# Odd heads of a two-block kernel: outputs with tokens on partitions, and each head's gate row loaded instead of multiplied out

## The chip, the cores and the metric

The kernel runs on one core of one Trainium2 chip. The metric is the device time of one execution in microseconds; less is better. Engines are named as in the profile: PE is TensorE, DVE is VectorE, ACT is ScalarE, POOL is GpSimd, and SP issues most of the DMA transfers.

## The reference, cut to what matters

The whole kernel computes two transformer blocks, with a second block of an even and an odd layer. The change is in the odd layer, an mLSTM with 8 heads, 512 tokens in 4 chunks of 128, 128 channels for q and k and 256 for v. Per head and chunk:

```
b = cumsum(lf);  m_t = running maximum;  g_inter = exp(b + m_prev - m_t)
sc  = (q k^T) * exp(b_t - b_s + li_s - m_t), causal
num = g_inter * (q C) + sc v
den = g_inter * (q n) + sum_s sc
hout = num / max(|den|, exp(-m_t))
C, n = decay * C + kw^T v,  decay * n + sum kw
...
y = rmsnorm over the head's 256 channels(hout) * norm * sigmoid(og) * silu(z)
```

All of it is in fp32. `og`, `z`, `v`, `q`, `k` and the two gates come from one projection of the normalised input.

## The kernel before, in words

`odd_stage` runs the projection and the heads together. `Projection` (class in the same file) turns the weights into products: a job is 128 output columns over 16 row blocks, each with three fp32r products of 512 tokens (high times high, high times low, low times high), 48 products. Weights come in chunks of four row blocks, four chunks to such a job, through a ring of six slots: SP loads a chunk up to 12 chunks ahead, ACT makes its high part (`split_high`, L2400), DVE its low part (`split_low`, L2407), PE multiplies (L2384 to L2386). A slot is free again when PE has used it (`chunk_done`) and, for the raw weights, when the low part is made (`lo_set`).

The first 21 jobs (`EARLY`) make q, k, the gate rows and v, which go through DRAM. Then each head has four jobs, two for `og` and two for `z`, and PE's order of work is written out by hand: a job, then the head's first products, a job, the state products, a job, the output products, a job, the sums. So the head's own work on DVE, ACT and POOL has a job of PE's time to finish in.

In the head's first piece PE multiplies table columns, repeated by a step of zero, with the identity. That lays one row of the table over all partitions, in PSUM: `b - m` to bank 0 (L3996, `cum_ready`) and `m` to bank 1 (`m_ready`). ACT makes `grow` and `floor` from them, DVE `expo`. PE also turns k (L4001) and multiplies k with q (L4005). The state products (L4013, L4014) are 256 columns of v and 128 columns of ones for each of three chunks. The output products (L4024, L4026) put channels on partitions and 512 tokens on columns: one bank for the denominator, repeated on all partitions by a stationary `ones`, and two for the numerator. ACT and DVE make the denominator's absolute value, maximum and reciprocal on 128 x 512, and the quotient `o`; ACT squares it; PE sums the squares over the channels with two products with `ones` (L4040); ACT makes the inverse root, DVE multiplies by it and the norm, then by the gate that POOL made from `og` and `z`, and SP stores the head.

SP loads k, q and v of the next head during the current one (`load`, L3926 to L3928), into two buffers in turn. In the last head `tail.turn_p` and the tail's first weights are fitted between; the tail's (`Tail.tensor`) third embedding job waits until the head's banks 0 and 1 are free.

A table load on ACT (`preload_act_table_set` and before L2419) comes wherever the function changes between the set with exponential and logarithm and the sets with sigmoid and silu.

Of the kernel before, what the change touches and what calls it, by code (L numbers as in the profile page):

```python
# [1223 lines left out]
ML_SW = (ML_E + 1) * P  # L1224
# [2607 lines left out]
def odd_stage(nc, a, consts, cols, h, qk_dram, v_dram, y_dram, sum_sq, lead, following, p_tok, p_in, u, make_tail):  # L3832
# [8 lines left out]
    SW = ML_SW  # L3841
    GATE_JOB, EARLY, PER_HEAD = 2, 21, 4
    FIRST_LOAD, FIRST_MADE = 18, (0, 9, 17)
    ADD_BANK = (3, 0, 1)
    with ExitStack() as ctx:
# [9 lines left out]
        v_tok = [sb("v_tok0", ML_CH, ML_E * P)]  # L3855
        q_in, k_in = ([sb(f"{n}_in0", LAT)] for n in "qk")
        inv, inv_col, eps = sb("inv", LAT), sb("inv_col", ML_CH), sb("eps", 1)
        tabs = sb("tabs", ML_TABS, ML_CH, ML_H)
        og, z = sb("og", ML_E, LAT), sb("z", ML_E, LAT)
# [9 lines left out]
        for head in range(ML_H):  # L3869
            free = (y_set, head) if head > 0 else None  # L3870
# [16 lines left out]
        def rows8(name, *shape):  # L3887
# [11 lines left out]
        v_tok = [v_tok[0], sb("v_tok1", ML_CH, ML_E * P, owner=late)]  # L3899
        grow, expo, floor = sb("grow", ML_CH, P, owner=late), sb("expo", ML_CH, P, owner=late), sb("floor", LAT, owner=late)  # L3900
        score, k_w, state = sb("score", ML_CH, P, owner=late), sb("k_w", ML_CH, P, owner=late), sb("state", ML_CH - 1, SW, owner=late)
        den, o_sq, o, o_inv = sb("den", LAT, owner=late), sb("o_sq", ML_E, LAT, owner=late), sb("o", ML_E, LAT, owner=late), sb("o_inv", LAT, owner=late)
# [5 lines left out]
        cum_ready, m_ready, k_turned, kq_ready = sem("cum_ready"), sem("m_ready"), sem("k_turned"), sem("kq_ready")  # L3908
        grow_set, floor_set, expo_set, w_set = sem("grow_set"), sem("floor_set"), sem("expo_set"), sem("w_set")
        q_grown, k_w_set, score_set = sem("q_grown"), sem("k_w_set"), sem("score_set")  # L3910
        add_ready, state_set = sem("add_ready"), sem("state_set")
        den_ready, num_ready = sem("den_ready"), sem("num_ready")
        den_abs, den_max, den_inv, o_set = sem("den_abs"), sem("den_max"), sem("den_inv"), sem("o_set")
        o_squared, o_sums, o_ln, o_inv_set, y_normed, gate_set, y_gated = (sem(n) for n in (
            "o_squared", "o_sums", "o_ln", "o_inv_set", "y_normed", "gate_set", "y_gated"))
# [3 lines left out]
        def _(sp):  # L3919
# [4 lines left out]
            def load(hd):  # L3924
                b = hd % 2
                sp.dma_start(k_in[b][:], qk_dram[hd + ML_H]).then_inc(loaded[b], 16)  # L3926
                sp.dma_start(q_in[b][:], qk_dram[hd]).then_inc(loaded[b], 16)
                sp.dma_start(v_tok[b][:], v_view[:, :, ML_E * P * hd:ML_E * P * (hd + 1)]).then_inc(loaded[b], 16)  # L3928

            for n in range(EARLY):  # L3930
                proj.sp_upto(sp, KD * (n + 1))
                if n == FIRST_LOAD:
                    for made in FIRST_MADE:
                        proj.wait_job_stored(sp, made)
                    load(0)
                if n == GATE_JOB:
                    sp.wait_ge(proj.evacuated, n + 1)
                    for i in range(2):
                        sp.dma_start(raw_gates[:, i, :], gate_rows[112 + 8 * i:120 + 8 * i, :]).then_inc(gate_moved, 16)
            for hd in range(ML_H):  # L3940
                for j in range(PER_HEAD):
                    proj.sp_upto(sp, KD * (EARLY + PER_HEAD * hd + j + 1))
                    if j == 1 and hd < ML_H - 1:
                        if hd == 0:
                            proj.wait_stored(sp)
                        else:
                            sp.wait_ge(q_grown, hd)
                            sp.wait_ge(num_ready, ML_E * hd)
# [9 lines left out]
                sp.wait_ge(y_set, hd + 1)  # L3958
# [6 lines left out]
        def _(pe):  # L3965
# [19 lines left out]
            for hd in range(ML_H):  # L3985
# [25 lines left out]
                pe.wait_ge(floor_set, hd + 1)  # L4011
# [8 lines left out]
                for i, e, ready in ((2, ML_E, den_ready), (3, 0, num_ready), (0, 1, num_ready)):  # L4020
                    for c in range(ML_CH):
                        part = slice(c * P, (c + 1) * P)
                        if c > 0:
                            pe.matmul(bank[i][:, part], state[:, c - 1, e * P:(e + 1) * P], grow[:, c, :], start=True, stop=False)  # L4024
                        values = ones[:] if e == ML_E else v_tok[hd % 2][:, c, e * P:(e + 1) * P]
                        last = pe.matmul(bank[i][:, part], values, score[:, c, :], start=(c == 0), stop=True)  # L4026
                    last.then_inc(ready, 1)
# [15 lines left out]

        @block.scalar
        def _(act):
            norm.act(act)
            for n in range(EARLY):
# [9 lines left out]
                if n == GATE_JOB + 6:  # L4057
                    act.wait_ge(gate_n, 15)
                    act.preload_act_table_set(EXP_LN)
                    act.activation(tabs[:, 4:6, :, :], tabs[:, 4:6, :, :], ACT.Exp).then_inc(tabs_set, 1)  # L4060

            for hd in range(ML_H):
# [3 lines left out]
                act.wait_ge(cum_ready, hd + 1)  # L4066
                if hd > 0:
                    act.wait_ge(num_ready, ML_E * hd)
# [11 lines left out]
                act.wait_ge(den_ready, hd + 1)  # L4080
                act.activation(den[:], bank[2][:, :], ACT.Abs).then_inc(den_abs, 1)
                if hd == ML_H - 1:
                    tail.p_high(act, 0, bank[1])
                act.wait_ge(o_set, ML_E * (hd + 1))
                act.activation(o_sq[:], o[:], ACT.Square).then_inc(o_squared, 1)
                if hd == ML_H - 1:
                    tail.p_high(act, 1, bank[1])
# [710 lines left out]
```

## Time and profile before

| | us |
|---|---|
| median of 3 runs | 3729.44 |
| lowest, highest run | 3723.15, 3731.35 |
| profiled execution, span from first to last instruction | 3723.4 |
| the eight odd heads in it | 2878 to 3325 |

For the profiled execution no other time than its span is given. An fp32 product appears in the trace as two records of PE, and a transpose as one. The records' lengths overlap, since products are pipelined, so the cost of a product is the distance between starts, or its part of the chain that ended last. "Idle before" is the time in which an engine did nothing before an instruction, and the arrow names what released it.

### The profile page before, as it was taken

To read this page: it belongs to the slowest core of one execution; us is meant where nothing else is said; L and a number is where in the kernel's file an instruction comes from. 1 tells how busy PE (TensorE), PEld (TensorE's weight loads), DVE (VectorE), ACT (ScalarE), POOL (GpSimd) and SP (SyncE) were. 2 spreads that over 40 slices of the span, in tenths; PEclk is the share of its full clock that TensorE was granted. 3 is DMA by queue.
4 is the path that set the end of the run, shared out by engine and by line. 5 is a ranking of instruction groups with operands and counts; after the bars stand their busy time and mean duration, and the time that the engine had idled before them with its cause. 6 is when DMAs were issued, how large, how long until landed. Compare 5 with 4: busy or idle time off the path is not lost. (4 is left out here: it accounts for less than half of the span.)

```text
span 3723.4 us, 49664 instructions
## 1 busy us (share of the span) xinstructions
PE 3550.2 (95%) x19794; PEld 2945.9 (79%) x19794; DVE 1956.4 (53%) x2995; ACT 1512.3 (41%) x2540; POOL 422.1 (11%) x346
## 2 busy tenths in 40 slices
PE   6999999899878889999999999999999999999998
PEld 3688888777667777888888788888888888888886
DVE  7555554466578545645555554445533444454543
ACT  3322222255646543556565532333322444452332
POOL 1000000044000000001011160120000000024021
PEclk8999999999989999999999999999999999999999
DMA  9743333322544354422322253335634555543332
GB/s 358 264 141 127 112 106 107 93 79 80 173 127 119 96 171 133 145 83 79 94 86 88 79 176 96 95 79 115 132 116 122 125 95 112 105 133 102 94 94 88
DMA packets 580504, 448.37 MB, mean 120 GB/s; under 512 B 64454, under 2 KB 500114, under 8 KB 579504
## 3 DMA queue, kind: packets, MB, share of 16 engines
q1 hardware_dynamic: 570416, 420.98, 40.3%
q10 hardware_dynamic: 7712, 19.34, 1.3%
q0 software_dynamic: 2144, 4.87, 0.4%
q8 instruction: 157, 2.57, 0.3%
q14 instruction: 75, 0.61, 0.1%
HBM read 387.61 MB, written 57.46 MB: 120 GB/s over the span
## 5 line engine op out<-in xcount | busy, mean ns | idle before, releaser
L2407 DVE TENSOR_TENSOR w_lo<-w,w_hi 128x512 fp32r<-128x512 f32 x429 | 291.4, 698 | 499.7 <-ACT w_hi L2400 499.7
L2400 ACT ACTIVATE w_hi<-w 128x512 fp32r<-128x512 f32 x429 | 261.0, 625 | 478.5 <-PE od_acc L2386 179.0
L4539 DVE TENSOR_TENSOR w_lo<-w,w_hi 128x512 fp32r<-128x512 f32 x260 | 232.2, 899 | 353.3 <-ACT w_hi L4432 351.9
L4398 PE MATMUL ta_acc<-u_hi,w_hi 128*128 128x512 f32 x960 | 375.2, 391 | 2.7 <-POOL u_lo L4333 1.4
L4400 PE MATMUL ta_acc<-u_hi,w_lo 128*128 128x512 f32 x960 | 373.7, 389 | 0.0
L4399 PE MATMUL ta_acc<-u_lo,w_hi 128*128 128x512 f32 x960 | 373.5, 389 | 0.0
L4432 ACT ACTIVATE w_hi<-w 128x512 fp32r<-128x512 f32 x260 | 163.5, 630 | 440.4 <-PE ta_acc L4400 435.0
L2384 PE MATMUL od_acc<-u_hi,w_hi 128*128 128x512 f32 x768 | 304.7, 397 | 0.0
L2386 PE MATMUL od_acc<-u_hi,w_lo 128*128 128x512 f32 x768 | 299.3, 390 | 0.0
L2385 PE MATMUL od_acc<-u_lo,w_hi 128*128 128x512 f32 x768 | 299.0, 389 | 0.0
L2384 PE MATMUL ev_acc<-u_hi,w_hi 128*128 128x512 f32 x608 | 250.7, 412 | 13.7 <-DVE w_lo L2407 5.1
L2386 PE MATMUL ev_acc<-u_hi,w_lo 128*128 128x512 f32 x608 | 239.2, 393 | 0.0
L2385 PE MATMUL ev_acc<-u_lo,w_hi 128*128 128x512 f32 x608 | 239.1, 393 | 0.0
L1969 PE MATMUL p_acc<-u_hi,p_w_hi 128*128 128x512 f32 x544 | 216.9, 399 | 2.5 <-DVE p_w_lo L1777 2.5
L1976 PE MATMUL p_acc<-u_hi,p_w_lo 128*128 128x512 f32 x544 | 216.9, 399 | 0.0
L4398 PEld LDWEIGHTS ta_acc<-u_hi,w_hi 128*128 128x128 f32 x960 | 180.2, 188 | 43.0 <-DVE u_lo L4547 3.0
L1970 PE MATMUL p_acc<-u_lo,p_w_hi 128*128 128x512 f32 x544 | 213.3, 392 | 0.0
L4400 PEld LDWEIGHTS ta_acc<-u_hi,w_lo 128*128 128x128 f32 x960 | 180.2, 188 | 37.8
L4399 PEld LDWEIGHTS ta_acc<-u_lo,w_hi 128*128 128x128 f32 x960 | 180.2, 188 | 37.7 <-issue 0.5
L2113 DVE TENSOR_TENSOR p_w_lo<-p_w,p_w_hi 128x1024 fp32r<-128x1024 f32 x66 | 80.6, 1224 | 225.9 <-ACT p_w_hi L2015 225.9
L2015 ACT ACTIVATE p_w_hi<-p_w 128x1024 fp32r<-128x1024 f32 x66 | 69.7, 1060 | 249.7 <-PE p_acc L1976 179.9
L2385 PEld LDWEIGHTS od_acc<-u_lo,w_hi 128*128 128x128 f32 x768 | 144.3, 188 | 30.9 <-issue 1.9
(754 smaller groups left out, 7973.2 us busy)
## 6 DMA issues: line engine op xcount, KB each, us to landing
w<-in_o_w_in_dram SPq DMA_DIRECT2D x260, 256.0 KB, 6.7
w<-in_e_w_in_dram SPq DMA_DIRECT2D x144, 256.0 KB, 2.9
p_w<-in_w_in_dram SPq DMA_DIRECT2D x70, 512.0 KB, 6.1
mod_w<-in_w_ada_dram SPq DMA_DIRECT2D x32, 1024.0 KB, 11.4
w<-in_ple_gate_w_dram SPq DMA_DIRECT2D x128, 256.0 KB, 2.7
gate_w<-in_w_ada_dram SPq DMA_DIRECT2D x16, 1024.0 KB, 5.9
z_w<-in_w_in_dram SPq DMA_DIRECT2D x64, 256.0 KB, 3.0
w<-in_e_w_out_dram SPq DMA_DIRECT2D x64, 256.0 KB, 2.7
```

Of the source, the lines that this page charges most:

```text
L1969: pe.matmul(lat, wh, x_hi[:, k, :], start=first, stop=False)
L1970: pe.matmul(lat, wh, x_lo[:, k, :], start=False, stop=False)
L1976: last = pe.matmul(lat, wl, x_hi[:, k, :], start=False, stop=end)
L2384: pe.matmul(out, hi, self.x_hi[:, k, :], start=first, stop=False)
L2385: pe.matmul(out, hi, self.x_lo[:, k, :], start=False, stop=False)
L2386: last = pe.matmul(out, lo, self.x_hi[:, k, :], start=False, stop=end)
L2400: act.activation(self.w_hi[m % self.ring][:], self.w[m % self.ring][:], ACT.Copy).then_inc(self.hi_set, 1)
L2407: eng.tensor_tensor(self.w_lo[m % self.ring][:], self.w[m % self.ring][:], self.w_hi[m % self.ring][:].bitcast(F32), ALU.subtract).then_in ...
L4398: pe.matmul(bank, hi, hi_x[:, k, :], start=(k == 0), stop=False)
L4399: pe.matmul(bank, hi, lo_x[:, k, :], start=False, stop=False)
L4400: last = pe.matmul(bank, lo, hi_x[:, k, :], start=False, stop=(k == job.kd - 1))
L4539: dve.tensor_tensor(self.w_lo[m % RING][:], self.w[m % RING][:], self.w_hi[m % RING][:].bitcast(F32), ALU.subtract).then_inc(self.lo_set, 1)
```

## The change

The output products change sides: `grow` and `score` are stationary, and the state or v with one column of ones (`SW` = 257) is moving. Their results have tokens on partitions, one bank to a chunk (`NUM_BANK`), the denominator in column 256. The denominator's maximum and reciprocal are then on one column a chunk; ACT squares and sums along the row in one instruction a chunk, and the inverse root is on four columns. DVE scales each chunk into `y_tok`, PE turns it back (8 transposes), and DVE multiplies by the norm and the gate out of PSUM. The state products take the column of ones with v. The rows `b - m` are stored to DRAM once, and each head's row is loaded repeated over the partitions (`cum_in`) with k, q and v. `floor` is made once for all heads. `turn_p` in the last head uses the projection's banks, the gate on POOL is made in two halves, and the tail's third embedding job waits for the last head's `y_set`; the tail's second `embed_odd_out` moves behind it.

```diff
--- before.py
+++ after.py
...
-ML_SW = (ML_E + 1) * P
+ML_SW = ML_E * P + 1
...
+    NUM_BANK = (2, 3, 0, 1)
...
-        v_tok = [sb("v_tok0", ML_CH, ML_E * P)]
+        v_tok = [sb("v_tok0", ML_CH, SW)]
...
+        cum_in = [sb("cum_in0", LAT)]
+        cum_dram = nc.dram_tensor("s_cum3", (ML_H, LAT), F32).ap()
...
+        y_tok, squares = sb("y_tok", ML_CH, ML_E * P, owner=late), sb("squares", ML_CH, ML_E * P, owner=late)
...
             def load(hd):
                 b = hd % 2
+                sp.dma_start(cum_in[b][:], cum_dram[hd:hd + 1, :].to_broadcast([P, LAT])).then_inc(loaded[b], 16)
...
+                sp.dma_start(v_tok[b][:, :, 0:ML_E * P], v_view[:, :, ML_E * P * hd:ML_E * P * (hd + 1)]).then_inc(loaded[b], 16)
...
+                    sp.wait_ge(cum_stored, 16)
...
+                if n == GATE_JOB + 4:
+                    sp.wait_ge(gate_n, 8)
+                    sp.dma_start(cum_dram[:, :], rows[:, 0, :]).then_inc(cum_stored, 16)
...
-                else:
-                    pe.wait_ge(o_set, ML_E * hd)
-                    pe.wait_ge(o_ln, hd)
-                for i, t, ready in ((0, 0, cum_ready), (1, 2, m_ready)):
-                    for c in range(ML_CH):
-                        last = pe.matmul(bank[i][:, c * P:(c + 1) * P], tabs[:, t, c, hd:hd + 1].to_broadcast([P, P]),
-                                         ident[:], start=True, stop=True)
-                    last.then_inc(ready, 1)
...
-                pe.wait_ge(loaded[hd % 2], 48 * (hd // 2 + 1))
+                pe.wait_ge(loaded[hd % 2], 64 * (hd // 2 + 1))
...
+                if hd > 0:
+                    pe.wait_ge(y_set, ML_E * hd)
                 for c, i in enumerate(ADD_BANK):
-                    pe.matmul(bank[i][:, 0:ML_E * P], k_w[:, c, :], v_tok[hd % 2][:, c, :], start=True, stop=True)
-                    pe.matmul(bank[i][:, ML_E * P:SW], k_w[:, c, :], ones[:], start=True, stop=True).then_inc(add_ready, 1)
+                    pe.matmul(bank[i][:, 0:SW], k_w[:, c, :], v_tok[hd % 2][:, c, :], start=True, stop=True).then_inc(add_ready, 1)
...
+                for c, i in enumerate(NUM_BANK):
+                    if c > 0:
+                        pe.matmul(bank[i][:, 0:SW], grow[:, c, :], state[:, c - 1, :], start=True, stop=False)
+                    pe.matmul(bank[i][:, 0:SW], score[:, c, :], v_tok[hd % 2][:, c, :], start=(c == 0), stop=True).then_inc(num_ready, 1)
...
-                        if f > 0:
-                            pe.wait_ge(tail.p_set, f)
-                        tail.turn_p(pe, f, bank[1])
+                        tail.turn_p(pe, f, proj.acc[f][1])
                         proj.pe_steps(pe, KD // 2)
-                    pe.wait_ge(tail.p_set, 2)
-                pe.wait_ge(o_squared, hd + 1)
+                pe.wait_ge(y_tok_set, ML_CH * (hd + 1))
                 for e in range(ML_E):
-                    last = pe.matmul(bank[1][:, :], ones[:], o_sq[:, e, :], start=(e == 0), stop=(e == ML_E - 1))
-                last.then_inc(o_sums, 1)
-            tail.tensor(pe, None, (o_ln, ML_H))
+                    for c in range(ML_CH):
+                        last = pe.transpose(bank[e][:, c * P:(c + 1) * P], y_tok[:, c, e * P:(e + 1) * P], ident[:])
+                    last.then_inc(y_turned, 1)
+            tail.tensor(pe, None, (y_set, ML_E * ML_H))
...
+                    act.activation(floor[:], tabs[:, 2, :, :], ACT.Exp, scale=-1.0).then_inc(floor_set, 1)
...
-                act.wait_ge(cum_ready, hd + 1)
+                act.wait_ge(loaded[hd % 2], 64 * (hd // 2 + 1))
...
-                    ins = act.activation(grow[:, c, :], bank[0][:, c * P:(c + 1) * P], ACT.Exp, bias=tabs[:, 7, c, hd:hd + 1])
+                    ins = act.activation(grow[:, c, :], cum_in[hd % 2][:, c * P:(c + 1) * P], ACT.Exp, bias=tabs[:, 7, c, hd:hd + 1])
                 ins.then_inc(grow_set, 1)
-                act.wait_ge(m_ready, hd + 1)
-                act.activation(floor[:], bank[1][:, :], ACT.Exp, scale=-1.0).then_inc(floor_set, 1)
...
-                act.wait_ge(den_ready, hd + 1)
-                act.activation(den[:], bank[2][:, :], ACT.Abs).then_inc(den_abs, 1)
...
+                    tail.p_high(act, 0, proj.acc[0][1])
+                act.preload_act_table_set(EXP_LN)
+                act.wait_ge(den_inv, hd + 1)
+                if hd > 0:
+                    act.wait_ge(scale_set, hd)
+                for c, i in enumerate(NUM_BANK):
+                    ins = act.activation(squares[:, c, :], bank[i][:, 0:ML_E * P], ACT.Square, scale=den[:, c:c + 1], accum_out=y_sq[:, c:c + 1])
+                ins.then_inc(squared, 1)
+                act.wait_ge(squared, hd + 1)
+                act.activation(y_scale[:], y_sq[:], ACT.Ln, scale=1.0 / (ML_E * P), bias=eps[:, 0:1]).then_inc(y_ln, 1)
+                act.wait_ge(y_ln, hd + 1)
+                act.activation(y_scale[:], y_scale[:], ACT.Exp, scale=-0.5).then_inc(y_inv_set, 1)
...
-                act.preload_act_table_set(EXP_LN)
-                act.wait_ge(o_sums, hd + 1)
-                act.activation(o_inv[:], bank[1][:, :], ACT.Ln, scale=1.0 / (ML_E * P), bias=eps[:, 0:1]).then_inc(o_ln, 1)
-                act.wait_ge(o_ln, hd + 1)
-                act.activation(o_inv[:], o_inv[:], ACT.Exp, scale=-0.5).then_inc(o_inv_set, 1)
...
+                for e in range(ML_E):
+                    pool.wait_ge(proj.finished, proj.finish_no[EARLY + PER_HEAD * hd + 2 + e])
+                    pool.tensor_tensor(z[:, e, :], og[:, e, :], z[:, e, :], ALU.mult).then_inc(gate_set, 1)
...
-                dve.tensor_tensor(expo[:], bank[0][:, :].rearrange("p (c t) -> p c t", c=ML_CH),
+                dve.tensor_tensor(expo[:], cum_in[hd % 2][:].rearrange("p (c t) -> p c t", c=ML_CH),
...
-                dve.wait_ge(den_abs, hd + 1)
-                dve.tensor_tensor(den[:], den[:], floor[:], ALU.max).then_inc(den_max, 1)
...
+                for c, i in enumerate(NUM_BANK):
+                    dve.wait_ge(num_ready, ML_CH * hd + c + 1)
+                    ins = dve.tensor_scalar(den[:, c:c + 1], bank[i][:, ML_E * P:SW], floor[:, c, hd:hd + 1], None, ALU.max)
+                ins.then_inc(den_max, 1)
+                dve.wait_ge(den_max, 2 * hd + 1)
+                for c, i in enumerate(NUM_BANK):
+                    ins = dve.scalar_tensor_tensor(den[:, c:c + 1], bank[i][:, ML_E * P:SW], -1.0, den[:, c:c + 1], ALU.mult, ALU.max)
+                ins.then_inc(den_max, 1)
+                dve.wait_ge(den_max, 2 * hd + 2)
+                dve.reciprocal(den[:], den[:]).then_inc(den_inv, 1)
                 if hd == ML_H - 1:
-                    tail.p_low(dve, 0, bank[1])
-                dve.wait_ge(den_max, hd + 1)
-                dve.reciprocal(den[:], den[:]).then_inc(den_inv, 1)
...
+                    tail.p_low(dve, 0, proj.acc[0][1])
+                dve.wait_ge(y_inv_set, hd + 1)
+                dve.tensor_tensor(y_scale[:], y_scale[:], den[:], ALU.mult).then_inc(scale_set, 1)
+                dve.wait_ge(scale_set, hd + 1)
+                for c, i in enumerate(NUM_BANK):
+                    dve.tensor_scalar(y_tok[:, c, :], bank[i][:, 0:ML_E * P], y_scale[:, c:c + 1], None, ALU.mult).then_inc(y_tok_set, 1)
...
-                    tail.embed_odd_out(dve, 1)
-                dve.wait_ge(o_inv_set, hd + 1)
+                dve.wait_ge(stored, 16 * hd)
                 for e in range(ML_E):
-                    ins = dve.scalar_tensor_tensor(o[:, e, :], o[:, e, :], norm_w[:, ML_E * hd + e:ML_E * hd + e + 1], o_inv[:],
-                                                   ALU.mult, ALU.mult)
-                ins.then_inc(y_normed, 1)
-                dve.wait_ge(y_normed, hd + 1)
-                dve.wait_ge(gate_set, hd + 1)
-                dve.tensor_tensor(o[:], o[:], z[:], ALU.mult).then_inc(y_set, 1)
+                    dve.wait_ge(y_turned, ML_E * hd + e + 1)
+                    dve.wait_ge(gate_set, ML_E * hd + e + 1)
+                    dve.scalar_tensor_tensor(o[:, e, :], bank[e][:, :], norm_w[:, ML_E * hd + e:ML_E * hd + e + 1], z[:, e, :],
+                                             ALU.mult, ALU.mult).then_inc(y_set, 1)
+            tail.embed_odd_out(dve, 1)
```

## Rows read from the trace of the kernel before

**Rows 1.** The page's head and its first part: engine, busy us, share, instructions.

```profile
span 3723.4 us, 49664 instructions
...
PE 3550.2 (95%) x19794; PEld 2945.9 (79%) x19794; DVE 1956.4 (53%) x2995; ACT 1512.3 (41%) x2540; POOL 422.1 (11%) x346
```

**Rows 2.** Busy table by stretches: us, busy us, granted clock (PEclk), DMA share, GB/s.

```profile
2999.16:3054.30 55.14, 55.14 (x279) 46.42 (x278) 24.70 (x33) 24.28 (x38) 3.69 (x2) 1.00 0.52 103
2878.00:3325.00 447.00, 447.00 (x2255) 376.23 (x2254) 200.11 (x269) 194.39 (x306) 29.50 (x16) 1.00 0.54 112
```

**Rows 3.** PE's waits in the eight heads, 2880 to 3330 us.

```profile
PE ta_acc L4398 <- ACT od_o_inv L4095: 0.5, 1, 0.5
```

**Rows 4.** The chain that ended last, one head: start us, us, what.

```profile
2999.32 1.78 PE od_bank L3996 x16
3001.10 0.44 PE od_bank L4001 x4
3001.54 0.89 PE od_bank L4005 x8
...
3003.13 0.23 PE od_acc L2384
...
3013.36 0.43 PE od_bank L4013 x2
3014.01 0.43 PE od_bank L4013 x2
...
3041.82 1.72 PE od_bank L4040 x4
```

**Rows 5.** PE's timeline, the output products' first record and the products after them.

```profile
3026.06 0.38 PE L4026 MATMUL od_bank<-od_score,k_ones 128*128 128x128 f32 x2
...
3030.98 0.39 PE L2385 MATMUL od_acc<-u_lo,w_hi 128*128 128x512 f32 x1
```

**Rows 6.** PE's groups in the heads, output products: xcount, busy us, mean ns.

```profile
L4024 PE MATMUL od_bank<-od_grow,od_state 128*128 128x128 f32 x144 | 27.8, 275 | 0.0
L4026 PE MATMUL od_bank<-od_score,od_v_tok 128*128 128x128 f32 x128 | 23.4, 275 | 0.0
...
L4026 PE MATMUL od_bank<-od_score,k_ones 128*128 128x128 f32 x64 | 12.3, 274 | 0.0
```

**Rows 7.** VectorE's groups by shape, small operations out of PSUM, whole span.

```profile
L2459 DVE TENSOR_SCALAR ev_v_tok<-ev_acc,ev_inv_col 128x256 f32<-128x256 f32 x12 | 5.0, 476 | 0.0
...
L1607 DVE TENSOR_TENSOR vec<-mod_cols_p,cols 128x4 f32<-128x4 f32 x8 | 1.3, 163 | 13.1 <-PE mod_cols_p L1382 12.9
```

**Rows 8.** ScalarE's timeline around the output products of the same head.

```profile
3026.96 1.28 ACT L2419 ACT_TABLE_LOAD   x1
3028.30 0.63 ACT L2419 ACTIVATE od_z<-od_z 128x512 f32<-128x512 f32 x1
```

**Rows 9.** ScalarE's groups by shape, small operations, whole span.

```profile
L804 ACT ACTIVATE gdn_v_new<-gdn_bank 128x256 f32<-128x256 f32 x32 | 10.5, 388 | 10.6 <-PE gdn_bank L588 10.6
...
L3605 ACT ACTIVATE ev_decay_end<-h 128x4 f32<-128x4 f32 x8 | 1.5, 191 | 0.0
```

**Rows 10.** Timelines of SP's queue and ScalarE; DMA issues, KB, median us to landing.

```profile
2908.90 2.13 SPq L3926 DMA_DIRECT2D od_k_in<-s_qk  x1
...
2904.04 0.63 ACT L2400 ACTIVATE w_hi<-w 128x512 fp32r<-128x512 f32 x1 [4.80 <-DMA w<-in_o_w_in_dram]
...
w<-in_o_w_in_dram SPq DMA_DIRECT2D x260, 256.0 KB, 6.7
...
od_k_in<-s_qk SPq DMA_DIRECT2D x8, 256.0 KB, 6.5
```

**Rows 11.** Timelines of PE and VectorE where the tail begins.

```profile
3326.20 0.50 PE L4398 MATMUL ta_acc<-ta_p_hi,w_hi 128*128 128x512 f32 x1 [0.49 <-ACT od_o_inv L4095]
...
3324.18 0.69 DVE L2205 TENSOR_TENSOR w_lo<-w,w_hi 128x512 fp32r<-128x512 f32 x1 [0.46 <-ACT w_hi L2200]
...
3326.84 1.42 DVE L4197 SCALAR_TENSOR_TENSOR od_o<-od_o,cols,od_o_inv 128x512 f32<-128x512 f32 x2 [0.41 <-ACT od_o_inv L4097]
```

More of the change, by code:

```diff
@@ L3869, in odd_stage @@
         for head in range(ML_H):
-            free = (y_set, head) if head > 0 else None
+            free = (y_set, ML_E * head) if head > 0 else None
             for base, tile, func in ((4096, og, ACT.Sigmoid), (6144, z, ACT.Silu)):
@@ L3898, in odd_stage @@
         q_in, k_in = ([tiles[0], sb(f"{n}_in1", LAT, owner=late)] for n, tiles in (("q", q_in), ("k", k_in)))
-        v_tok = [v_tok[0], sb("v_tok1", ML_CH, ML_E * P, owner=late)]
-        grow, expo, floor = sb("grow", ML_CH, P, owner=late), sb("expo", ML_CH, P, owner=late), sb("floor", LAT, owner=late)
+        v_tok = [v_tok[0], sb("v_tok1", ML_CH, SW, owner=late)]
+        grow, expo = sb("grow", ML_CH, P, owner=late), sb("expo", ML_CH, P, owner=late)
         score, k_w, state = sb("score", ML_CH, P, owner=late), sb("k_w", ML_CH, P, owner=late), sb("state", ML_CH - 1, SW, owner=late)
-        den, o_sq, o, o_inv = sb("den", LAT, owner=late), sb("o_sq", ML_E, LAT, owner=late), sb("o", ML_E, LAT, owner=late), sb("o_inv", LAT, owner=late)
+        cum_in = [cum_in[0], sb("cum_in1", LAT, owner=late)]
+        y_tok, squares = sb("y_tok", ML_CH, ML_E * P, owner=late), sb("squares", ML_CH, ML_E * P, owner=late)
+        o = sb("o", ML_E, LAT, owner=late)
         bias_in, gate_moved = sem("bias_in"), sem("gate_moved")
@@ L3907, in odd_stage @@
         loaded, stored = [sem("loaded0"), sem("loaded1")], sem("stored")
-        cum_ready, m_ready, k_turned, kq_ready = sem("cum_ready"), sem("m_ready"), sem("k_turned"), sem("kq_ready")
+        cum_stored, k_turned, kq_ready = sem("cum_stored"), sem("k_turned"), sem("kq_ready")
         grow_set, floor_set, expo_set, w_set = sem("grow_set"), sem("floor_set"), sem("expo_set"), sem("w_set")
+        ones_set = sem("ones_set")
         q_grown, k_w_set, score_set = sem("q_grown"), sem("k_w_set"), sem("score_set")
         add_ready, state_set = sem("add_ready"), sem("state_set")
[L3912 to L3915, printed above, removed]
+        num_ready = sem("num_ready")
+        den_max, den_inv, squared, y_ln, y_inv_set = (sem(n) for n in (
+            "den_max", "den_inv", "squared", "y_ln", "y_inv_set"))
+        scale_set, y_tok_set, y_turned, gate_set = sem("scale_set"), sem("y_tok_set"), sem("y_turned"), sem("gate_set")
         block = ctx.enter_context(nc.Block())
@@ L4019, in _ @@
                 pe.wait_ge(state_set, 3 * (hd + 1))
[L4020 to L4027, printed above, removed]
+                for c, i in enumerate(NUM_BANK):
+                    if c > 0:
+                        pe.matmul(bank[i][:, 0:SW], grow[:, c, :], state[:, c - 1, :], start=True, stop=False)
+                    pe.matmul(bank[i][:, 0:SW], score[:, c, :], v_tok[hd % 2][:, c, :], start=(c == 0), stop=True).then_inc(num_ready, 1)
                 if hd < ML_H - 1:
@@ L4079, in _ @@
                 proj.act_upto(act, KD * (job + 3))
-                act.wait_ge(den_ready, hd + 1)
-                act.activation(den[:], bank[2][:, :], ACT.Abs).then_inc(den_abs, 1)
                 if hd == ML_H - 1:
-                    tail.p_high(act, 0, bank[1])
-                act.wait_ge(o_set, ML_E * (hd + 1))
-                act.activation(o_sq[:], o[:], ACT.Square).then_inc(o_squared, 1)
+                    tail.p_high(act, 0, proj.acc[0][1])
[10 more added lines that the diff above has]
+                act.activation(y_scale[:], y_scale[:], ACT.Exp, scale=-0.5).then_inc(y_inv_set, 1)
                 if hd == ML_H - 1:
-                    tail.p_high(act, 1, bank[1])
+                    tail.p_high(act, 1, proj.acc[1][1])
                     following.split_high(act, proj.chunk_done, following.first)
@@ L4107, in _ @@
                                    ALU.mult).then_inc(q_grown, 1)
-                pool.wait_ge(proj.finished, proj.finish_no[EARLY + PER_HEAD * hd + 3])
-                pool.tensor_tensor(z[:], og[:], z[:], ALU.mult).then_inc(gate_set, 1)
+                for e in range(ML_E):
+                    pool.wait_ge(proj.finished, proj.finish_no[EARLY + PER_HEAD * hd + 2 + e])
+                    pool.tensor_tensor(z[:, e, :], og[:, e, :], z[:, e, :], ALU.mult).then_inc(gate_set, 1)
             tail.gpsimd(pool)
@@ L4114, in _ @@
             norm.dve(dve)
+            dve.memset(v_tok[0][:, :, ML_E * P:SW], 1.0).then_inc(ones_set, 1)
             done = [0]
@@ L4175, in _ @@
                 proj.dve_upto(dve, KD * (job + 3))
-                dve.wait_ge(den_abs, hd + 1)
-                dve.tensor_tensor(den[:], den[:], floor[:], ALU.max).then_inc(den_max, 1)
-                if hd == ML_H - 1:
-                    tail.p_low(dve, 0, bank[1])
-                dve.wait_ge(den_max, hd + 1)
-                dve.reciprocal(den[:], den[:]).then_inc(den_inv, 1)
-                dve.wait_ge(den_inv, hd + 1)
-                dve.wait_ge(stored, 16 * hd)
-                for e, i in ((0, 3), (1, 0)):
-                    dve.wait_ge(num_ready, ML_E * hd + e + 1)
-                    dve.tensor_tensor(o[:, e, :], bank[i][:, :], den[:], ALU.mult).then_inc(o_set, 1)
+                if hd > 0:
+                    dve.wait_ge(squared, hd)
+                else:
+                    proj.wait_stored(dve)
+                    dve.memset(v_tok[1][:, :, ML_E * P:SW], 1.0).then_inc(ones_set, 1)
+                    dve.wait_ge(floor_set, 1)
+                for c, i in enumerate(NUM_BANK):
[8 more added lines that the diff above has]
+                dve.reciprocal(den[:], den[:]).then_inc(den_inv, 1)
+                if hd == ML_H - 1:
+                    tail.p_low(dve, 0, proj.acc[0][1])
[4 more added lines that the diff above has]
+                    dve.tensor_scalar(y_tok[:, c, :], bank[i][:, 0:ML_E * P], y_scale[:, c:c + 1], None, ALU.mult).then_inc(y_tok_set, 1)
                 if hd == ML_H - 1:
-                    tail.p_low(dve, 1, bank[1])
+                    tail.p_low(dve, 1, proj.acc[1][1])
                     following.split_low(dve, following.first)
```

15 lines of the change are left out of this document (8 added, 7 removed).

## The prediction

> **What bounds the kernel now.** I read the page's first part, the busy table of the stretch with the odd heads, PE's waits there, the chain that ended last, and only then the other engines. The page gives a span of 3723.4 us with PE busy for 95% of it [rows 1]. A share over the whole span says nothing about the stage that changes, so the table by stretches comes next: from 2878 to 3325 us PE is busy for 447.00 of 447.00 us, at a granted clock of 1.00, the upper level (2.4 GHz) [rows 2]. One head takes 55.14 us, in which VectorE (DVE) works 24.70 us and ScalarE (ACT) 24.28 us [rows 2]. The list of PE's waits has one entry for all eight heads, 0.5 us, at the hand-over to the tail [rows 3]. So in this stage TensorE's program order is the path: a microsecond taken from its list is a microsecond of the kernel, as long as no new wait appears; and what VectorE and ScalarE do is free until it makes PE wait.
>
> **What PE does for one head.** Each head has four projection jobs of 48 products, and between them four pieces of its own. The chain gives what each piece holds of the path, with an fp32 product counted as two records: the 8 products with the identity take 1.78 us, the 4 transposes of k 0.44 us, the 4 products k·q 0.89 us [rows 4]. The three state products follow one another at 0.65 us (3013.36, 3014.01), 0.43 for 256 columns and so 0.22 for the 128 of `ones` [rows 4]. The output products begin at 3026.06 and the second projection product after them at 3030.98; less the 0.23 us of the first [rows 4] that makes 4.69 us [rows 5]. Their records are 144 + 128 + 64 = 336 in eight heads, 21 products a head, 0.223 us each [rows 6]. The two sums over 512 columns take 1.72 us [rows 4]. All own pieces: 3.11 + 1.95 + 4.69 + 1.72 = 11.47 us; the four jobs are the rest of 55.14, that is 43.67 or 10.92 each.
>
> **The change on PE, step by step.** (1) The identity products go: 1.78 us. (2) State products: six become three of 257 columns. A pair over 256 columns costs 0.43; one more column in proportion costs 0.002, so 3 x 0.43 = 1.30 instead of 1.95: 0.65 saved. (3) Output products: 21 of 128 columns become 7 of 257: 7 x 0.433 = 3.03 instead of 4.69: 1.66 saved. (4) The two sums give way to 8 transposes. Four cost 0.44, so eight cost 0.88 instead of 1.72: 0.84 saved. Together 1.78 + 0.65 + 1.66 + 0.84 = 4.93 us a head, 39.4 us for eight.
>
> Two prices are not in the trace. No product has 257 columns: at best the odd column is free, at worst it costs like a further product of 128 columns, 0.22, which on ten products a head is 2.2 us, 17.6 us in all. I take the low end: rows of 128 and 256 columns are proportional to the columns, 0.22 and 0.43. The new transposes read `y_tok` and not `k_in`, with the same shape, type and identity; at worst they cost like the products with the identity, 1.78 / 8 = 0.22 each, 0.9 us a head or 7.2 in all. I take the k rows, which are the same operation.
>
> **The change on the other engines, and what hides it.** PE next needs the result of the output products after one projection job: it waits for `y_tok_set` 3.03 + 10.92 = 13.95 us after the output products begin. Counted from that start: the last denominator is there at 3.03. VectorE then does one of its four maxima (the first three are done while PE works), four more and a reciprocal, all on one or four columns; the nearest row, 4 columns with one operand from PSUM, is 163 ns [rows 7]: 6 x 0.16 = 1.0, so 4.0. ScalarE: the Silu before it ended at 3028.30 + 0.63 = 3028.93, 2.87 after the start, and a table load takes 1.28: ready at 4.15 [rows 8]. Four squares over 256 columns from PSUM: 0.39 each by the nearest row [rows 9]; the row sums that they also write out have no row, from nothing to one more small operation, 0.19 [rows 9]. That gives 1.6 to 2.3 us. Logarithm and exponential over four columns 0.19 each, VectorE's product 0.16, four scalings of 256 columns out of PSUM 0.48 each [rows 7, 9]: the chain ends between 8.2 and 9.0; some seven hand-overs at 0.1 make it 9.7 at most. Slack: over 4 us. So the whole chain costs nothing; past that slack each microsecond costs 8 us. The rows show a fixed part per operation: 0.163 us for 4 columns against 0.476 for 256 [rows 7].
>
> The Trainium skill, "VectorE: DVE Perf Modes", section "The TRN2 errata — SBUF-src ops pay a fixed extra latency per instruction", speaks against this part: it advises tiles of 512 elements or more because each instruction pays a fixed cost (for PSUM operands 120 cycles on VectorE, 172 on ScalarE), and the change puts many small operations where few large ones were. By its formula, with the clocks of the same table, a 256-column square is an estimated 0.36 us and a one-column VectorE operation 0.13, so the chain would end no later than by the rows, and the sum is the same by both; where the rule would bite, the chain past its slack, it is the third rival.
>
> Weight splitting on both engines gets at most this added: ScalarE 1.28 + 2.3 + 0.4 = 4.0 us a head, VectorE 9 x 0.16 + 0.16 + 4 x 0.48 = 3.5, with nothing taken off for what goes. That is 28.3 and 28.2 us in a head of 55.14 - 4.93 = 50.2. Six chunk slots are split ahead when the output products begin, and PE needs the seventh after 3.03 + 10.92 + 0.88 and two more chunks (a job has four) of 2.73, at 20.3; ScalarE is back before 8, VectorE before 10. Hidden.
>
> The gate row load is one more transfer on SP's queue, first in each head's load, ahead of k, q and v, and weight loads are queued behind them. Issuing k held the queue for 2.13 us in the first head [rows 10]; I take the same for the row. Weights are issued up to 12 chunks, 12 x 2.73 = 32.8 us, ahead of their use, and land in a median of 6.7 [rows 10], so 2.13 us more is covered. The second head's row is asked for near 2909 [rows 10] and needed with k at that head's first piece, 2999.16 - 55.14 = 2944.02 [rows 2]: 35 us, against a median landing of 6.5 for k, of the same size in SBUF [rows 10]. In the first head ScalarE waited 4.80 us for a weight [rows 10]; PE did not wait then [rows 3], and that cover stays. The extra DMA of the eight rows, the two small fills of ones and the table of floors come before the heads' path: nothing.
>
> **The end of the stage.** The tail's third embedding product now waits for the finished last head instead of the logarithm. Today PE loses 0.49 us there [rows 11]. In the new order VectorE multiplies twice behind the split that starts at 3324.18: 3324.18 + 0.69, two operations of 1.42 in sum as today's pair [rows 11], 3326.3, all 0.84 earlier with PE. PE, ready at 3326.20 - 0.49 = 3325.7 today, is so 0.84 earlier as well: it waits some 0.6 to 0.9 us. I charge 0.4 more than today.
>
> **Sum.** 39.4 - 0.4 = 39.0 us. The profiled execution has a span of 3723.4, and the fastest of three runs is 3723.15, so nothing measurable lies around the span: its own time becomes 3723.4 - 39.0 = 3684.4. The median of the runs shown, 3729.44, lies 6.0 above it; I forecast a median: 3690.4. A change of 0.2%, 7.5 us, is about what the runs shown can tell from none.
>
> **Rivals.** First, the odd column costs a product of its own: 39.0 - 17.6 = 21.4 saved, 3708. For it: 257 columns occur nowhere in the rows. Against it: cost in proportion at 128, 256 and 512 columns (1.72 for four records of 512) [rows 4].
>
> Second, the new transposes do not run in one pass: 39.0 - 7.2 = 31.8 saved, 3697.6. Against it: 32 records of that operation at 0.11 us.
>
> Third, the other side: the chain from the last output product to `y_tok` is late, and PE stands at `y_tok_set` in every head. It decides from 13.95 us on, and the kernel is slower than before once the chain ends past 13.95 + 4.88 = 18.8. At 20 the wait is 6 us a head and the time 3690.4 + 48 = 3738. For it: it crosses between the two engines five times, with a table load in it. Against it: 9.7 by rows, half of what it takes.
>
> Fourth, the change moves PE's list without shortening the stage, because weights then bound it: PE would wait for chunks, at most until the old period is back, 3729. Half of that is 3710. For it: the 4.80 us [rows 10] and DMA engines busy 0.52 to 0.54 of the time [rows 2]. Against it: both splitting engines stay under 60%.
>
> **Chances.** Forecast 0.72; odd column 0.08; transposes 0.08; weights 0.08, of which 0.03 ends within 0.2% of before; late chain 0.04, of which 0.03 is slower. That makes faster 0.93, same 0.04, slower 0.03. The range goes from 3680, the spread of the runs shown (6 us below the median) and some more below the forecast, to 3708, the odd column: it holds all but the late chain and the worse part of the weights' case.
>
> **What would show it.** Right: a head of 50.2 us with PE at its full share, 257-column pairs 0.433 apart, eight transposes in 0.88, no entry for `y_tok` among PE's waits, and VectorE's last scaling of a head 4 us or more before the transposes. Wrong: pairs at 0.5 or more (odd column), a granted clock under 1.00 in the heads, PE idle before the transposes or before a projection product with ScalarE or a DMA as releaser.

## The result, and the profile after

The changed kernel takes 3686.55 us (median of 4 runs, 3683.49 to 3688.23) against 3728.83 for the kernel before on the same chip: ratio 0.9882, 95% interval 0.9868 to 0.9896, that is 39 to 49 us less. Forecast were 3690.4 us and 39.0 us less; the time lies in the range. The profiled execution took 3688.23 us with a span of 3686.4.

The page's head of the kernel after, which answers to [rows 1]:

```profile
span 3686.4 us, 49077 instructions
...
PE 3511.6 (95%) x19426; PEld 2912.0 (79%) x19426; DVE 1924.1 (52%) x3069; ACT 1517.0 (41%) x2589; POOL 428.0 (12%) x354
```

The busy table by stretches: most of the eight heads, and the first head alone (columns as in [rows 2]).

```profile
2880.00:3290.00 410.00, 409.62 (x1897) 341.88 (x1895) 171.01 (x346) 200.57 (x357) 34.27 (x24) 1.00 0.64 126
2892.72:2942.89 50.17, 50.17 (x234) 41.92 (x233) 20.67 (x43) 24.78 (x44) 4.32 (x3) 1.00 0.70 150
```

PE is still full in a head, at the upper clock, and a head takes 50.17 us instead of 55.14 [rows 2]: 4.97 less, 39.8 for eight. The chain that ended last, one head, says of what:

```profile
2892.72 0.44 PE od_bank L4005 x4
2893.16 0.89 PE od_bank L4009 x8
2904.96 1.30 PE od_bank L4020 x6
2917.16 0.43 PE od_bank L4029 x2
2917.59 0.43 PE od_bank L4028 x2
...
2919.76 0.43 PE od_bank L4029 x2
2931.11 0.87 PE od_bank L4040 x8
2942.89 0.44 PE od_bank L4005 x4
```

The identity products are gone, the state products (L4020) take 1.30 us, the seven output products follow one another at 0.43 (3.03 in all), and eight transposes (L4040) take 0.87, against 1.78, 1.95, 4.69 and 1.72 [rows 4, 5]. PE's waits from 2880 to 3300 us have one entry, and it isn't for `y_tok`: the wait that stood in [rows 3], with a new releaser and its old length:

```profile
PE ta_acc L4411 <- DVE od_o L4213: 0.5, 1, 0.5
```

The chain to `y_tok` in the third head, whose output products begin at 3017.34, on VectorE:

```profile
3020.57 0.22 DVE L4187 TENSOR_SCALAR od_den<-od_bank,od_floor 128x1 f32<-128x1 f32 x1 [0.64 <-PE od_bank L4029]
3020.82 0.35 DVE L4191 SCALAR_TENSOR_TENSOR od_den<-od_bank,od_den 128x1 f32<-128x1 f32 x4
3021.21 0.18 DVE L4194 RECIPROCAL od_den<-od_den 128x4 f32<-128x4 f32 x1
3024.06 0.16 DVE L4198 TENSOR_TENSOR od_y_scale<-od_y_scale,od_den 128x4 f32<-128x4 f32 x1 [2.67 <-ACT od_y_scale L4091]
3024.26 1.66 DVE L4201 TENSOR_SCALAR od_y_tok<-od_bank,od_y_scale 128x256 f32<-128x256 f32 x4
```

and on ScalarE, the table load, the first of four squares with the read of its row sum, the second, and the logarithm:

```profile
3020.23 1.28 ACT L4081 ACT_TABLE_LOAD   x1
3021.53 0.48 ACT L4086 ACTIVATE od_squares<-od_bank,od_den 128x256 f32<-128x256 f32 x1
3021.90 0.19 ACT L4086 ACTIVATION_READ_ACCUMULATOR od_squares<-od_bank,od_den 128x1 f32 x1
3021.99 0.47 ACT L4086 ACTIVATE od_squares<-od_bank,od_den 128x256 f32<-128x256 f32 x1
...
3023.49 0.30 ACT L4089 ACTIVATE od_y_scale<-od_y_sq,od_eps 128x4 f32<-128x4 f32 x1
```

`y_tok` is done at 3025.92, 8.6 us after the output products began; PE's transposes start at 3031.28, 13.9 after. The slack is 5.4 us.

The spans differ by 37.0 us. From the start of the heads' own work to the tail it is 39.8 less (431.19 before, 391.41 after), and the tail is 0.9 shorter; but the heads begin 3.7 us later than before (2892.72 against 2889.03). The second profile of the same kernel (below) shows how far the stretch ahead of the heads scatters.

### The profile page after: what moved, and what is told of

Read it like the earlier page. It is cut to its first block and busy times, and to the rows that moved or that the text cites. A ratio compares the mean times of both kernels' runs of the same rounds, so it can differ in the third digit from the quotient of the medians.

```text
span 3686.4 us, 49077 instructions
## 1 busy us (share of the span) xinstructions
PE 3511.6 (95%) x19426; PEld 2912.0 (79%) x19426; DVE 1924.1 (52%) x3069; ACT 1517.0 (41%) x2589; POOL 428.0 (12%) x354
## 5 line engine op out<-in xcount | busy, mean ns | idle before, releaser
L2386 PEld LDWEIGHTS od_acc<-u_hi,w_lo 128*128 128x128 f32 x768 | 144.1, 188 | 30.3
```

The source lines that it names most:

```text
L2386: last = pe.matmul(out, lo, self.x_hi[:, k, :], start=False, stop=end)
```

## Experiments

Ratios are to the kernel before, on the same chip; the changed kernel has 0.9882, and 0.9888 when it ran again. They are known to some 0.0014, 5 us; the head's period, read from the chain between two starts of the k transposes, is known to some hundredths of a us and decides where the ratio can't.

**The gate row undone alone.**

```diff
-                sp.dma_start(cum_in[b][:], cum_dram[hd:hd + 1, :].to_broadcast([P, LAT])).then_inc(loaded[b], 16)
...
+                if hd > 0:
+                    pe.wait_ge(y_set, ML_E * hd)
+                for i, t in ((0, 0), (1, 2)):
+                    for c in range(ML_CH):
+                        last = pe.matmul(bank[i][:, c * P:(c + 1) * P], tabs[:, t, c, hd:hd + 1].to_broadcast([P, P]),
+                                         ident[:], start=True, stop=True)
...
```

ScalarE and VectorE read the row from PSUM again.

> The kernel after, with one part undone: the gate row is not loaded; the eight products with the identity stand on TensorE again (the four of the cum row are read, the other four have no reader), and nothing else differs. Theory (a piece taken from TensorE's list is worth its place on the chain, and the row's load was covered): 1.78 us a head come back, the head goes from 50.17 to 51.95 us, eight heads +14.2 us against the kernel after, and TensorE still has no wait in the heads. Rival (SP's queue or the DMA engines were a hidden price of the load): the missing 256 KB a head give something back, so less than +12 us. Second rival (part of the products was in time in which TensorE could not go on anyway): head under 51.5 us.

Measured: 3704.28 us, ratio 0.9924 (0.9912 to 0.9937), 0.0042 or 16 us above the changed kernel. The chain, one head and the next one's first piece:

```profile
2894.80 1.78 PE od_bank L4006 x16
2896.59 0.44 PE od_bank L4012 x4
...
2946.77 1.78 PE od_bank L4006 x16
```

A head of 51.97 us, 1.80 more, 14.4 for eight. The theory holds and both rivals fall: the products are worth their whole length, and the load that replaces them gives nothing back when it is left out.

**Columns: 320 and 256 instead of 257.**

The first kernel:

```diff
-ML_SW = ML_E * P + 1
+ML_SW = ML_E * P + 64
...
```

The second, which leaves out the column of ones; its denominators read v's last column:

```diff
-ML_SW = ML_E * P + 1
+ML_SW = ML_E * P
...
```

> The kernel after, with 64 columns of ones behind the 256 of v instead of one: the ten state and output products of a head move 320 columns, and only one of the 64 sums is read. Theory (cost in proportion to the columns): a pair goes from 0.433 to 0.540 us, ten of them +1.07 us, the head 51.24 us, +8.5 us in all. Rival (cost in steps of 128 columns, the odd column rival of the prediction): 0.65 a pair, +2.2 us a head, +17.4 us in all. Second rival (a product of this size is set by its weights' load and not by the columns): no change, 50.2 us a head.

> The kernel after without the column of ones: 256 columns a product, the denominator is taken from v's last column instead of the sum, so the values differ. Theory (the odd column costs its share, 0.002 us): a pair 0.432 instead of 0.433, the head 50.15 us, -0.1 us in all, not measurable. Rival (an odd number of columns, or columns past 256, carry a price of their own): the pair is shorter by more than 0.01 us, the head by more than 0.1 us and the kernel by 1 us or more; at 0.05 us a pair it would be 4 us.

Measured: 3696.15 us, ratio 0.9906 (0.9891 to 0.9921) with 320 columns; 3691.47 us, 0.9888 (0.9874 to 0.9901) with 256. The chain with 320:

```profile
2892.20 0.44 PE od_bank L4005 x4
...
2904.45 1.62 PE od_bank L4020 x6
2916.99 0.54 PE od_bank L4029 x2
2917.53 0.54 PE od_bank L4028 x2
...
2943.46 0.44 PE od_bank L4005 x4
```

and with 256:

```profile
2918.26 0.43 PE od_bank L4027 x2
2918.69 0.43 PE od_bank L4026 x2
...
2943.98 0.44 PE od_bank L4005 x4
...
2994.21 0.44 PE od_bank L4005 x4
```

The pair of records that makes one product goes from 0.43 to 0.54, the head to 51.26: from 257 to 320 columns the cost is in proportion, without a step of 128, and the columns, not the weights, set it. With 256 the head is 50.23, no shorter than with 257. The odd column is free within what the trace resolves.

**Transposes as plain products.**

```diff
-                        last = pe.transpose(bank[e][:, c * P:(c + 1) * P], y_tok[:, c, e * P:(e + 1) * P], ident[:])
+                        last = pe.matmul(bank[e][:, c * P:(c + 1) * P], y_tok[:, c, e * P:(e + 1) * P], ident[:], start=True, stop=True)
```

> The kernel after, with the eight transposes of y_tok as plain products of y_tok with the identity, same operands and same banks. Theory (a transpose is one pass, a plain fp32 product of 128 columns two): 0.11 us more for each, the eight take 1.75 instead of 0.87 us, the head 51.04, +7.0 us in all. Rival (the price of 0.11 us is that of a short product behind another, whatever its mode): no change, 50.2 us a head. VectorE's two products that follow are later by the same 0.9 us and hidden.

Measured: 3697.84 us, ratio 0.9907 (0.9894 to 0.9921). The chain:

```profile
2932.73 1.79 PE od_bank L4040 x16
2945.41 0.44 PE od_bank L4005 x4
...
2996.49 0.43 PE od_bank L4005 x4
```

Sixteen records instead of eight, 1.79 us instead of 0.87, a head of 51.08. With the same operands and banks the mode of the instruction makes the price; a plain product is what the prediction's second rival would have had to pay.

**The gate row three times.**

```diff
+                for r in range(2):
+                    sp.dma_start(spare[r][:], cum_dram[hd:hd + 1, :].to_broadcast([P, LAT])).then_inc(loaded[b], 16)
```

> The kernel after, with each head's gate row loaded three times, twice into tiles that nobody reads, ahead of k, q and v on the same queue. Theory (the row's load is covered by the lead of the weights and of the head's own loads): SP's queue is held 3 us longer a head, the head stays at 50.2 us, no change in all, no new wait of TensorE. Rival (weights or the head's loads bound the stage once PE's list is shorter, the fourth rival of the prediction): TensorE waits for a chunk or for the head's load, the head longer by up to the 3 us, 2 to 24 us in all.

Measured: 3690.57 us, ratio 0.9884 (0.9869 to 0.9899). The busy table of its second head:

```profile
2942.09:2992.25 50.16, 50.16 (x234) 41.94 (x233) 20.66 (x42) 24.78 (x44) 4.03 (x3) 1.00 0.64 134
```

PE is full and the head is as short as before the edit, though SP's queue spends 4.17 us more on the two extra rows:

```profile
3006.44 0.97 SPq L3934 DMA_DIRECT2D od_cum_in<-s_cum  x1
3007.45 4.17 SPq L3936 DMA_DIRECT2D od_spare<-s_cum  x2
```

The load is covered with room to spare; neither the queue nor the weights bound the stage.

**The changed kernel again.**

> The kernel after, unchanged, as the measure for the others on this chip and for what a profile of the same kernel scatters. Theory (the change saves 40.7 us between the first head and the end, and the rest of the difference of the two profiles is scatter ahead of the heads): a head of 50.17 us again and 391.4 us from the first k transposes to the tail, while the start of the heads lies anywhere within some 4 us of 2892.7. Rival (the change made something ahead of the heads slower, 3.7 us): the heads start at 2892.7 or later, and 3 us or more later than in any profile of the kernel before.

Measured: 3692.28 us (3690.97 to 3697.53), before 3733.9 on that chip, ratio 0.9888 (0.9871 to 0.9904). The chain:

```profile
2900.45 0.44 PE od_bank L4005 x4
2950.62 0.44 PE od_bank L4005 x4
...
3291.86 0.23 PE ta_acc L4411
```

The head takes 50.17 us to the hundredth, and from the first k transposes to the tail it is 391.41, as in the first profile (2892.72 to 3284.13). But the heads begin 7.7 us later than there, outside the 4 us that the theory allowed, and 11.4 later than in the one profile of the kernel before, as the rival asked. In the profile of the kernel with six groups of squares (below), whose instructions ahead of the heads are the same, they begin at 2888.96. So the place where the heads begin scatters by 11.5 us, and single profiles can't show or exclude a loss of 3.7. The medians speak against the rival: with such a loss the kernel would gain 37.0 us, and the gain of the first comparison, 42.3 us, has an interval (39 to 49) that excludes it; the second, 41.6, has a wider one (36 to 48) that doesn't.

The busy table shows where these two executions part. Up to 1000 us PE has run 5275 records in the first and 5273 in the second; then, in the first and in the second:

```profile
1000.00:1500.00 500.00, 423.88 (x3776) 357.05 (x3777) 303.83 (x606) 253.93 (x531) 12.09 (x22) 0.94 0.45 129
1000.00:1500.00 500.00, 420.54 (x3719) 354.14 (x3720) 299.15 (x596) 252.13 (x528) 12.04 (x22) 0.91 0.45 128
```

The second falls 57 records behind, 7.5 us at the first one's 7.55 records a us, at a lower granted clock. Why the clock differs there is open.

**A longer chain to `y_tok`.** Four kernels make the head's four squares n + 1 times, for n = 2, 3, 4, 5:

```diff
+                for r in range(n + 1):
                     for c, i in enumerate(NUM_BANK):
                         ins = act.activation(squares[:, c, :], bank[i][:, 0:ML_E * P], ACT.Square, ..., accum_out=y_sq[:, r, c:c + 1])
                     ins.then_inc(squared, 1)
+                    act.wait_ge(squared, (n + 1) * hd + r + 1)
...
```

> The kernel after, with the four squares of each head made three times, each group behind the one before, so that the chain from the output products to y_tok is longer; only the first group's sums are used. In the trace after, a group takes 1.9 us with its hand-over, and the chain ended 8.6 us after the output products began, 5.4 us ahead of the transposes at 13.94. Theory (a chain within its slack costs nothing): it ends near 12.4, the head stays at 50.2 us, no change, and y_tok does not enter TensorE's waits. Rival (ScalarE's added 3.8 us a head delay the splitting of weights): TensorE waits for chunks, a head over 50.5 us, 2 us or more in all.

> The same with six groups of squares instead of one. Theory (past the slack each microsecond of the chain is paid in every head, the third rival of the prediction): the chain ends near 8.6 + 9.5 = 18.1, the transposes come 4.1 us late, the head takes 54.3 us, eight heads +33 us (30 to 36), y_tok stands in TensorE's waits eight times, and the kernel is back near the time before. Rival (the splitting of weights falls behind as well): a head over 55.5 us, with waits for chunks beside those for y_tok. Second rival (the transposes are not bound to y_tok that late): less than +25 us.

Measured: n = 2: 3692.5 us, ratio 0.9892 (0.9877 to 0.9906), no change. The output products of the first head begin at 2925.73, and `y_tok` ends 12.5 us later:

```profile
2936.57 1.66 DVE L4202 TENSOR_SCALAR od_y_tok<-od_bank,od_y_scale 128x256 f32<-128x256 f32 x4
```

PE doesn't wait for it, and the head is 50.15 and 50.22 us in the first two. That part of the theory holds. n = 5: 3747.88 us, ratio 1.0036 (1.0022 to 1.0050), slower than the kernel before and 55.6 us above the changed kernel on that chip, where 33 were expected. PE's waits show no chunk, and little more waiting than expected, 4.4 us a head where 4.1 was:

```profile
PE od_bank L4040 <- DVE od_y_tok L4202: 35.2, 8, 4.8
```

Yet the heads take 56.93 us on the mean (2888.96 to 3287.49 is seven). The busy table of the first head's wait and of the stretch behind it, and the chain there:

```profile
2927.32:2931.72 4.40, 0.05 (x2) 0.00 (x1) 1.88 (x6) 4.34 (x14) 0.00 (x0) 0.84 0.00 0
2931.72:2937.43 5.71, 5.71 (x18) 4.91 (x19) 4.24 (x7) 2.05 (x3) 1.27 (x1) 0.52 0.62 128
```

```profile
2931.72 1.97 PE od_bank L4040 x8
2933.69 0.43 PE od_acc L2384
...
2937.43 0.23 PE od_acc L2384
```

Behind a wait of 4.40 us the granted clock is 0.52, close to the lower of TensorE's levels (1.2 GHz where 1.00 is 2.4), the transposes take 1.97 us and projection products stand 0.43 apart until 2937.43. Eight waits of 4.4 and some 2.4 us of slower products behind each make 54. Three more kernels test that, two with shorter waits and one with n = 5 whose wait is filled in seven heads:

```diff
+                if hd < ML_H - 1:
+                    stay_busy(pe, proj.acc[0][1], ones, 20)
                 pe.wait_ge(y_tok_set, ML_CH * (hd + 1))
```

> The kernel after with four groups of squares a head instead of one. With six groups TensorE stood 4.40 us a head for y_tok, but a head took 56.93 us on the mean, 6.76 more than 50.17; in the stretch behind the wait the granted clock was 0.52 in the first head, and products came 0.43 us apart. Two groups fewer (1.96 us each) leave a wait of some 0.4 to 0.5 us. Theory (the lower clock is the price of standing for some us, not of any wait): head 50.6 us, granted clock 1.00 behind the wait, +3.6 us on the kernel after. Rival (any wait at this place costs the 2.4 us of the slower products): head 52.9 us or more, +22 us.

> The same with five groups: a wait of 2.4 us a head. Where the price of the wait is its length alone: head 52.55 us, +19 us. Where the whole loss of the case with six groups comes with it (2.36 us of slower products a head): head 54.9 us, +38 us. Theory: the loss shrinks with the wait, so between the two, with a granted clock under 1.00 behind the wait in some heads.

> The kernel with six groups of squares, and in seven of the eight heads twenty products of the constant ones (128 columns, 0.22 us each, 4.4 us) on TensorE ahead of its wait for y_tok, into a bank that nobody reads; the last head is left as it was. y_tok is as late as with six groups alone. Theory (the 2.4 us a head beyond the wait's length are products at the lower clock, granted because TensorE stood idle): the clock stays at 1.00, the transposes take 0.87 us instead of 1.97, a filled head takes 54.6 to 54.8 us, and the kernel is 15 us faster than with six groups alone, for more products. Rival (the slow products behind the wait come from late weights or from ScalarE's and VectorE's load): a head stays at 56.9 us or gets longer.

Measured: n = 3: 3692.48 us, ratio 0.9898 (0.9883 to 0.9913). n = 4: 3722.55 us, 0.9983 (0.9973 to 0.9992). n = 5 filled: 3731.46 us, 1.0000 (0.9991 to 1.0009). The busy table of the first head with n = 3, and of the 6 us behind its wait:

```profile
2894.36:2945.18 50.82, 50.37 (x234) 41.85 (x233) 20.40 (x43) 30.36 (x68) 4.31 (x3) 1.00 0.63 139
2933.17:2939.17 6.00, 6.00 (x31) 5.11 (x32) 4.51 (x8) 2.83 (x4) 1.29 (x1) 1.00 0.61 121
```

with n = 4, the second and the third head:

```profile
2946.16:2999.01 52.85, 50.44 (x235) 41.88 (x233) 20.39 (x42) 32.18 (x76) 4.01 (x3) 1.00 0.46 111
2999.01:3053.41 54.40, 51.99 (x234) 43.26 (x233) 20.49 (x42) 32.18 (x76) 4.32 (x3) 0.97 0.73 112
```

and with n = 5 filled, the first head and the stretch behind the filler:

```profile
2892.99:2947.81 54.82, 54.82 (x275) 46.49 (x273) 20.40 (x43) 34.11 (x84) 4.32 (x3) 1.00 0.55 133
2935.87:2941.58 5.71, 5.71 (x30) 4.84 (x31) 4.22 (x8) 2.59 (x4) 1.29 (x1) 1.00 0.47 116
```

The last head of the same execution isn't filled; PE waits 4.8 us there, and the stretch behind that wait is

```profile
3322.02:3327.73 5.71, 5.71 (x18) 4.88 (x19) 4.15 (x7) 3.05 (x5) 0.82 (x1) 0.53 0.57 151
```

A wait of 0.45 us costs its length and 0.2 us more (the transposes take 1.09 instead of 0.87), with the clock at 1.00. A wait of 2.4 us, the same in both heads shown, came once at that price (52.85) and once with 1.55 us of slower products on top; six of the seven periods are 54.4 to 54.5, and the mean of the seven is 54.22. With the wait filled, `y_tok` is as late as with n = 5 (18.4 us after the output products began in both first heads) and ScalarE and VectorE work as much, but the clock stays at 1.00 and the first head takes 54.82; the mean of the seven filled heads is 54.98, with one of 55.7 in which `y_tok` came 1 us later still. That is 0.0036 in the ratio, 13 us where 15 were expected, back for 140 products more. In the last head, where PE stands idle again, the granted clock is 0.53 again. So the loss beyond the wait's length is the lower clock, and it comes from PE standing idle. The Trainium skill, "TensorE: Matmul & The Clock Gate", section "What's actually happening", has the low level as the default that activity lifts; the filled kernel agrees.

## Why the prediction was right, step by step

- **What bounds the stage.** PE's order was and stays the path: 50.17 of 50.17 us busy. The part that was undone, the gate row, came back with its whole length (1.80 us a head against 1.78). The state and output products weren't undone; their shares are read from the chains, and only their price by columns was tested.
- **The four terms.** Predicted 1.78, 0.65, 1.66 and 0.84, 4.93 a head; by the chains 1.78, 0.65, 1.66 and 0.85, and the period 4.97 shorter. For eight 39.8 us against 39.4.
- **The two unknown prices.** Both at the end taken: 257 columns 0.43 (256 and 320 measured beside it), eight transposes 0.87, plain products 1.79. The first two rivals are out.
- **The chain to `y_tok`.** Done at 8.6 us, inside the 8.2 to 9.7 worked out. Its parts differ a little: the row sums' reads put the squares 0.45 us apart where 0.39 and a read of up to 0.19 were taken; one-column operations on VectorE took 0.22 where 0.16 was taken and, four in a row, 0.35 in all. The prediction's second estimates, 0.36 for a square and 0.13 for a one-column operation, were too low as well. The 0.1 for a hand-over had no row; in this chain hand-overs took 0.02 to 0.04.
- **Cover.** Gate row and weights: no wait, with three rows a head either. The row held SP's queue 1.50 us in the third head, where 2.13 was taken. The fourth rival is out.
- **The end of the stage.** Charged at 0.4 us; PE idles 0.53 us against 0.49 [rows 11], so nothing. The prediction's own times (3326.3 less 3325.7, a wait of 0.6) gave 0.1 more than before, and it charged 0.4.
- **The total.** 42.3 us less in the medians, 39.8 in the heads; the interval (39 to 49) holds both, and the forecast at its edge. The difference of the two is the tail, 0.9 shorter where a loss was forecast, and scatter. Wrong was the sentence that nothing lies around the span: each run's time is its span plus 1.8 us, the same for both kernels, so it cancels. Right was to set the sum against the profiled execution and then move to the median: [rows 1] come from the fast end of the runs of before, the first profile after from the slow end of its own.
- **The third rival's price was wrong.** It was put at 8 us for each microsecond past the slack, with the turning point at 18.8 us. Waits of 2.4 and 4.4 us made a head 4.05 and 6.76 us longer, 1.5 to 1.7 for one. The kernel is back at the old time when a head is 4.97 longer, between `y_tok` at 16.4 us (ratio 0.9983) and at 18.4 (1.0036), on a straight line between the two at 17.1. The rival didn't occur, but it stood 8.5 us away from the measured 8.6 and not 10.2.

## What to carry to other kernels

Where PE's order is the path at full clock, count the records that a new layout removes and price them by columns and by mode: fewer products that also carry the sum in an extra column, and transposes instead of products with ones or the identity, gave what the rows said to 1% (4.97 us a head against 4.93). Before many small operations of other engines are put between two of PE's pieces, work out when the chain ends against when PE asks for it. Past that point a wait can cost more than its length: behind waits of 2.4 and 4.4 us the clock fell here, and products took longer.

## What the runs showed of the hardware

Behind waits of 2.4 us the granted clock fell in seven of the eight heads of one execution, behind waits of 0.4 to 0.9 us in none of the eight of another, and in the filled heads it stayed at 1.00. The row sum of a ScalarE square is an instruction of its own (0.19 to 0.21 us) that starts before the square's record ends, and the squares start 0.45 us apart. GpSimd's product of `q` and `grow`, the same in both kernels, took 1.70 us on the mean after and 1.29 before; nobody waits for it, and why wasn't tried.
